# Turning the second half's rows with VectorE in 32x32 blocks instead of TensorE transposes

## What is computed

```python
h = concatenate([meta, x])                                     # 16 meta tokens ahead of 2048
m = pool_mixer(h, a_w_in, a_w_group, a_scale, a_w_out)
h = layer_norm(ALPHA * h + m, ln_mix_g, ln_mix_b)
h = layer_norm(ALPHA * h + swiglu_ffn(h, ffn_w_gu, ffn_w_down), ln_ffn_g, ln_ffn_b)
return h[:, N_META:]

def swiglu_ffn(x, w_gu, w_down):
    gate, up = split(x @ w_gu, 2)      # 1024 -> 2816 each
    return (silu(gate) * up) @ w_down
```

## Time and profile before

| what | value |
|---|---|
| median of 3 runs | 1648.08 us |
| profiled execution | 1648.43 us |
| span of its instructions | 1646.5 us |
| TensorE busy | 1637.0 us (99%) |
| VectorE busy | 1036.0 us (63%) |
| GpSimd busy | 642.5 us (39%) |
| ScalarE busy | 620.9 us (38%) |
| mean granted TensorE clock | 0.999 of full |

### The profile page before, as it was taken

The page is one execution under the profiler, slowest core; times in us unless marked ns, Lnnn a source line. Parts: engine busy times, 40 slices in busy tenths (PEclk is TensorE's granted clock), DMA queues, the critical chain, the costliest instruction groups (busy, mean ns, idle before and its releaser), DMA issues.

```text
span 1646.5 us, 19031 instructions
## 1 busy us (share of the span) xinstructions
PE 1637.0 (99%) x7302; PEld 1354.2 (82%) x7302; DVE 1036.0 (63%) x1083; ACT 620.9 (38%) x844; POOL 642.5 (39%) x440
## 2 busy tenths in 40 slices
PE   9999999999999999999999999999999999999998
PEld 7888888888888888888888888888888888888886
DVE  6878885998445444454756677766643443467866
ACT  6334454445433433433533333333343332322330
POOL 0430025116357666654455666666621000341000
PEclk9999999999999999999999999999999999999999
DMA  9674467534467566565756666666577543564542
GB/s 361 250 284 154 152 252 261 193 141 177 120 212 239 190 209 224 181 198 192 243 181 222 216 211 192 203 209 200 176 222 275 188 146 131 196 223 173 197 146 95
DMA packets 190954, 330.84 MB, mean 201 GB/s; under 512 B 8464, under 2 KB 132496, under 8 KB 181136
## 3 DMA queue, kind: packets, MB, share of 16 engines
q1 hardware_dynamic: 151168, 297.64, 52.6%
q10 hardware_dynamic: 37520, 23.60, 4.7%
q0 software_dynamic: 2176, 8.39, 1.3%
HBM read 227.36 MB, written 102.24 MB: 200 GB/s over the span
## 4 chain that ended last, share of the span: by engine, by line
PE 97%; DVE 1%; DMA 0%; issue 0%; SPq 0%; ACT 0%; DVEq 0%
PE acc L1237 44%; PE acc L1269 19%; PE acc L1072 11%; PE turn L1237 7%; PE turn L1269 6%; PE acc L1106 6%; PE turn L1106 2%; PE acc L1136 1%; PE turn L1060 1%; PE acc L1149 0%; DMA raw<-w_out 0%; DVE fa L1846 0%; DVE split L1673 0%; DVE zm L1772 0%; DVE ring L1754 0%
## 5 line engine op out<-in xcount | busy, mean ns | idle before, releaser
L1237 PE MATMUL acc<-fa,wf 128*128 128x512 f32 x1584 | 366.1, 390 | 0.0
L1237 PE MATMUL acc<-fb,wf 128*128 128x512 f32 x1584 | 362.9, 389 | 0.0
L1237 PEld LDWEIGHTS acc<-fb,wf 128*128 128x128 f32 x1584 | 297.2, 188 | 62.0 <-issue 0.3
L1237 PEld LDWEIGHTS acc<-fa,wf 128*128 128x128 f32 x1584 | 296.1, 188 | 61.3 <-issue 0.2
L1269 PE MATMUL acc<-dw,da 128*128 128x512 f32 x1386 | 315.3, 389 | 0.0
L1269 PEld LDWEIGHTS acc<-dw,da 128*128 128x128 f32 x1386 | 260.1, 188 | 54.0
L1853 DVE TENSOR_TENSOR wf<-wt,wf 128x512 fp32r<-128x512 f32 x132 | 132.2, 1004 | 158.3 <-ACT wf L1442 158.2
L1853 DVE TENSOR_TENSOR wf<-wr,wf 128x512 fp32r<-128x512 f32 x176 | 171.8, 981 | 52.8 <-ACT wf L1442 52.5
L891 POOL TENSOR_TENSOR wt<-wr,wt 128x512 f32<-128x512 f32 x88 | 138.2, 1570 | 167.4 <-DVE wf L1853 167.3
L1442 ACT CAST wf<-wr 128x512 fp32r<-128x512 f32 x176 | 108.7, 618 | 212.5 <-PE acc L1237 200.6
L1947 DVE TENSOR_TENSOR da<-dar,da 128x1408 fp32r<-128x1408 f32 x56 | 91.9, 1642 | 136.3 <-ACT da L1556 136.3
(11 more groups left out here) (144 smaller groups left out, 1800.4 us busy)
## 6 DMA issues: line engine op xcount, KB each, us to landing
wr<-w_gu SPq DMA_DIRECT2D x44, 1024.0 KB, 5.2
dar<-af_dram SPq DMA_DIRECT2D x56, 704.0 KB, 4.3
af_dram<-g ACTq DMA_DIRECT2D x32, 512.0 KB, 5.7
raw<-w_in SPq DMA_DIRECT2D x15, 1024.0 KB, 7.0
fs<-hf_dram SPq DMA_DIRECT2D x14, 1024.0 KB, 5.9
dt_raw<-w_down SPq DMA_DIRECT2D x22, 512.0 KB, 5.6
wt_dram<-dt_t SPq DMA_DIRECT2D x22, 512.0 KB, 3.5
sa<-af_dram SPq DMA_DIRECT2D x22, 512.0 KB, 8.4
```

What stands on the lines that cost most here:

```text
L1237: mm = nc.tensor.matmul(dst, wf[:, slot, a, k, :], fa[half][i][:, v, :, k, :], start=i < 2 and k == 0 and n3 == 0, stop=k == KC - 1 and n3 ...
```

## The change

- The second half's rows are no longer transposed by TensorE. VectorE transposes them in blocks of 32x32 (`turn_rows`): four instructions of 128x512 elements for a pair, in the pair's first unit (5, 8, 11, 14), behind `unit_lo(n + 1, 0)` and, in an even unit, behind `up_out`. Each reads `nat_gu` with a step of 8 elements and writes straight into `st_gu`.
- A 32x32 transpose leaves a block on its own 32 partitions. So the rows are loaded such that partition group q holds column quarter q of 32 rows: 8 DMAs of 128 KB for a pair, with 1 KB pieces, in place of 2 of 512 KB with 4 KB pieces.
- The inner index that lands on a partition is then 8 * partition + chunk instead of 128 * chunk + partition. The host lays the gate and up weights and the norm's gain and bias out in that order (`by_chunks`). The first half is still transposed by TensorE, and reads its rows with a step of 8 elements, too (`pair_rows`).
- ScalarE's gain and bias are applied in place in `st_gu` (`scale_turned`), two activations of 128x256 at the same two places of the same units as `take_turn` had.
- `turn_rows` takes over the waits for the rows (`pair_landed`), for the store of the pair before (`st_stored`) and for its sums (`ss_made`).

```diff
--- before.py
+++ after.py
@@ -60,6 +60,9 @@
         return MIX0 + h * HALF_CHUNKS + 2 * PAIRS + t
 
     ADDS = HALVES * TT
+    Q = 32
+    QT = P // Q
+    assert QT == 4 and D // QT == KT * Q
 
     x_rows = x.rearrange("(n p) d -> p n d", p=P)
     h_rows = h_dram.rearrange("(n p) d -> p n d", p=P)
@@ -111,7 +114,7 @@
 
         st_mix = [at(f"st_mix{n}", R0 + off * KB, [P, 4, KC, P]) for n, off in enumerate((72, 88))]
         ss_mix = at("ss_mix", R0 + 96 * KB, [P, 4, KC, P])
-        nat_gu = at("nat_gu", N0, [P, 2, D])
+        nat_gu = at("nat_gu", N0, [P, 2, QT, D // QT])
         st_gu = at("st_gu", Z0, [P, 4, KC, P])
         ss_gu = at("ss_gu", Z0 + 8 * KB, [P, 4, KC, P])
 
@@ -373,11 +376,15 @@
         def st_of(pi):
             return st_mix[pi % 2] if pi < 4 else st_gu
 
-        def pair_rows(pi, a):
-
-            if pi >= TT:
-                return nat_gu[:, a]
-            return zm[a][:, pi]
+        def pair_rows(pi, a, kk):
+
+            return zm[a][:, pi].rearrange("p (r c) -> p c r", c=KT)[:, kk]
+
+        def turned_block(n):
+
+            a, kh = ((1, 0), (0, 0), (0, 1), (1, 1))[n]
+            src = nat_gu[:, a].rearrange("p g (r c) -> p g c r", c=KT)[:, :, kh * KC:(kh + 1) * KC]
+            return st_gu[:, n].rearrange("p k (g t) -> p g k t", t=Q), src
 
 
         HF_OF = (0, 3, 4, 1, 5, 6, 2)
@@ -561,9 +568,11 @@
                         for row in range(TT):
                             sp.wait_ge(rows_stored[e][row], 2 * 16)
                 else:
-                    sp.wait_ge(turn_done, 4 * pi)
+                    sp.wait_ge(turn_done, TT * pi)
+                src = h_dram.rearrange("(h a j g t) (q c) -> h j a g q t c", h=2, a=2, j=TT, g=QT, q=QT)[half, j]
                 for a in range(2):
-                    sp.dma_start(nat_gu[:, a, :], h_rows[:, half * 2 * TT + a * TT + j, :]).then_inc(pair_landed, 16)
+                    for n in range(QT):
+                        sp.dma_start(nat_gu[:, a, n], src[a, n]).then_inc(pair_landed, 16)
 
             def load_form(q):
                 half, i = form_of(q)
@@ -1047,18 +1056,12 @@
             def turn_part(pi, k):
 
                 part = TT * pi + k
-                if k == 0 and pi < TT:
+                if k == 0:
                     pe.wait_ge(normed, TT + pi + 1)
-                elif k == 0:
-                    pe.wait_ge(pair_landed, 32 * (pi - TT + 1))
-                slot = k % 2 if pi < TT else 1
-                if pi < TT and part >= 2:
+                if part >= 2:
                     pe.wait_ge(turn_taken, 2 * (part - 1))
-                elif pi >= TT:
-                    pe.wait_ge(turn_taken, 2 * part)
                 for n, (a, kk) in enumerate(((1, k), (0, k), (0, KC + k), (1, KC + k))):
-                    mm = nc.tensor.transpose(turn[:, slot, n * P:(n + 1) * P], pair_rows(pi, a)[:, kk * P:(kk + 1) * P],
-                                             ident[:])
+                    mm = nc.tensor.transpose(turn[:, k % 2, n * P:(n + 1) * P], pair_rows(pi, a, kk), ident[:])
                 mm.then_inc(turn_done, 1)
 
             def hidden(c, x_of, slot, banks, before=None, between=None):
@@ -1242,8 +1245,6 @@
             for n in range(UNITS):
                 for i in range(NP):
                     product(n, i)
-                    if turned_in(n)[0] is not None and i in (1, 4):
-                        turn_part(turned_in(n)[0], turned_in(n)[1] + i // 4)
 
             for k in range(DSTEPS):
                 t, m = k // MT, k % MT
@@ -1306,26 +1307,36 @@
                 if k == 0 and pi < 2:
 
                     act.wait_ge(d_lo_ready, NP)
-                if k == 0 and pi >= TT:
-                    act.wait_ge(st_stored[(pi - 1) % 2], 16 * ((pi + 1) // 2))
-                    act.wait_ge(ss_made, 4 * pi)
-                elif k == 0 and pi >= 2:
+                if k == 0 and pi >= 2:
 
                     act.wait_ge(st_stored[pi % 2], 16 * (pi // 2))
                     act.wait_ge(ss_made, 4 * (pi - 1))
-                slot = k % 2 if pi < TT else 1
                 if part == 0:
                     act.wait_ge(mix_gb_landed, 32)
 
                 for n, kk in enumerate((k, KC + k)):
                     nc.scalar.activation(st_of(pi)[:, 2 * n:2 * n + 2, k, :],
-                                         turn[:, slot, 2 * n * P:2 * (n + 1) * P].rearrange("p (b t) -> p b t", t=P),
+                                         turn[:, k % 2, 2 * n * P:2 * (n + 1) * P].rearrange("p (b t) -> p b t", t=P),
                                          ACT.Identity, bias=mix_b_sb[:, kk:kk + 1], scale=mix_g_sb[:, kk:kk + 1]
                                          ).then_inc(turn_taken, 1)
                 if k == KC - 1:
-                    act.wait_ge(turn_taken, 2 * (part + 1))
-                    nc.scalar.dma_start(pair_forms(pi)[:, 0:3, :], st_of(pi)[:, 1:4].rearrange("p f k t -> p f (k t)")
-                                        ).then_inc(st_stored[pi % 2], 16)
+                    store_turned(pi)
+
+            def store_turned(pi):
+                act.wait_ge(turn_taken, 2 * TT * (pi + 1))
+                nc.scalar.dma_start(pair_forms(pi)[:, 0:3, :], st_of(pi)[:, 1:4].rearrange("p f k t -> p f (k t)")
+                                    ).then_inc(st_stored[pi % 2], 16)
+
+            def scale_turned(pi, step):
+
+                kh, ks = step // 2, (2 * (step % 2), 2 * (step % 2) + 1)
+                act.wait_ge(turn_done, TT * pi + 2 * (kh + 1))
+                for k in ks:
+                    both, kk = st_gu[:, 2 * kh:2 * kh + 2, k, :], kh * KC + k
+                    nc.scalar.activation(both, both, ACT.Identity, bias=mix_b_sb[:, kk:kk + 1],
+                                         scale=mix_g_sb[:, kk:kk + 1]).then_inc(turn_taken, 1)
+                if step == 3:
+                    store_turned(pi)
 
             def stage_u(b, i):
                 act.wait_ge(chunk_done, c_in(b, i) + 1)
@@ -1599,7 +1610,7 @@
                     for j in LAST_ROWS[2 * (n - 2):2 * (n - 1)]:
                         norm(LAST, j)
                 if turned_in(n)[0] is not None:
-                    take_turn(turned_in(n)[0], turned_in(n)[1])
+                    scale_turned(turned_in(n)[0], turned_in(n)[1])
                 if n == 0:
                     unit_hi(1, 0)
                     unit_hi(1, 1)
@@ -1629,7 +1640,7 @@
                         down_w_hi(v)
                     act_form_hi(1)
                 if turned_in(n)[0] is not None:
-                    take_turn(turned_in(n)[0], turned_in(n)[1] + 1)
+                    scale_turned(turned_in(n)[0], turned_in(n)[1] + 1)
                 if gate:
                     act.wait_ge(c22_made, n + 1)
                     gate_out(jj, 3, g_of(jj)[:, 3, :])
@@ -1957,6 +1968,15 @@
                 if (n, place) in FORM_LO:
                     form_lo(FORM_LO[n, place])
 
+            def turn_rows(pi):
+
+                dve.wait_ge(pair_landed, 16 * 2 * QT * (pi - TT + 1))
+                dve.wait_ge(st_stored[(pi - 1) % 2], 16 * ((pi + 1) // 2))
+                dve.wait_ge(ss_made, 4 * pi)
+                for n in range(4):
+                    dst, src = turned_block(n)
+                    nc.vector.transpose(dst, src).then_inc(turn_done, 1)
+
             for n in range(UNITS):
                 jj, gate, nxt = n // 2, n % 2 == 0, n + 1 < UNITS
 
@@ -1966,6 +1986,8 @@
                 if n and gate:
                     dve.wait_ge(prod_done, NP * n)
                     up_out(jj - 1, 1, bank(n - 1, 1))
+                if turned_in(n)[1] == 0:
+                    turn_rows(turned_in(n)[0])
                 if n and nxt:
                     unit_lo(n + 1, 1)
                     new_form(n, 1)
@@ -2169,7 +2191,11 @@
     n_meta, ff, kt, cp = inputs["meta"].shape[0], inputs["ffn_w_down"].shape[1], d // P, CW // P
     jf = ff // (2 * P)
 
-    w_gu = np.asarray(inputs["ffn_w_gu"]).reshape(2, kt // 2, P, 2, 2, jf, P).transpose(0, 4, 5, 3, 2, 1, 6)
+    def by_chunks(a):
+
+        return np.asarray(a).reshape(P, 2, kt // 2, -1).transpose(1, 2, 0, 3)
+
+    w_gu = by_chunks(inputs["ffn_w_gu"]).reshape(2, kt // 2, P, 2, 2, jf, P).transpose(0, 4, 5, 3, 2, 1, 6)
 
     w_down = np.asarray(inputs["ffn_w_down"]).reshape(2, jf, P, 2, d // 2).transpose(0, 3, 2, 1, 4)
     arrays = {
@@ -2186,8 +2212,8 @@
         "w_out": lay(inputs["a_w_out"], (GROUPS, cp, P, d), (0, 2, 1, 3)),
         "mix_g": np.ascontiguousarray(inputs["ln_mix_g"][0]),
         "mix_b": np.ascontiguousarray(inputs["ln_mix_b"][0]),
-        "mix_gt": lay(inputs["ln_mix_g"], (kt, P), (1, 0)),
-        "mix_bt": lay(inputs["ln_mix_b"], (kt, P), (1, 0)),
+        "mix_gt": lay(by_chunks(inputs["ln_mix_g"]), (kt, P), (1, 0)),
+        "mix_bt": lay(by_chunks(inputs["ln_mix_b"]), (kt, P), (1, 0)),
 
         "w_gu": np.ascontiguousarray(blocks(w_gu).transpose(1, 2, 3, 0, 4, 5)),
```

## The result

The changed kernel takes 1660.82 us, the median of 6 runs (1660.33 to 1661.67), against 1648.32 us for the kernel before in its 6: ratio 1.0074, 95% interval 1.0064 to 1.0085. It is slower by 12.5 us, where 1641.0 was forecast. The profiled execution took 1660.33 us, its span is 1658.5 us (before: 1648.43 and 1646.5).

A forecast was written before the change was run, and what follows sets the result against it. TensorE, busy 1637.0 of 1646.5 us, was taken to bound the kernel. 1648.43 - 7.8 removed + 0.5 lateness = 1641.1 us, 1640.8 for the median, stated as 1641.0; range 1639.8 to 1650.0 us.

The forecast's parts named there:

- What bounds the kernel: Whole kernel: TensorE, busy 1637.0 of 1646.5 us, sets the time; other engines matter only through their dates.
- what is removed: TensorE's path: eight units lose their two parts of four transposes, 0.97 us each, 7.8 us in all.
- VectorE's transposes: Units 5, 8, 11, 14: four 128x512 transposes each, 0.7 to 1.2 us apiece, fit in VectorE's gaps.
- the seed's date: Product 4, 10.88 us into the unit, needs VectorE's seed; in time up to 1.76 (unit 5) or 1.18 us (unit 8) per transpose.
- 1.24 us for a transpose: VectorE: upper estimate from the skill's page for a 128x512 transpose; the sum about 0.8 us worse than at 0.7 us.
- The first half's transposes: TensorE: 64 transposes stay, now read with a step of 8; cost taken as nothing, upper bound 7.6 us.
- Rival B: TensorE: strided loads double the transposes' distance, 0.109 to 0.218 us; 7.0 us come back, 1648.0 us; chance 0.22.
- The rows' arrival: SP's eight loads: issues about 6.1 us, landing 4.4 us; pair 4 at 475.2 us, 2.8 us behind VectorE.
- all lateness: Units with VectorE's new work: 0.5 us in all allowed in the sum.
- Rival D: Row loads land late: pair 4 at 479.8 us, its seed 3.1 us late; 1643.6 us; chance 0.13.
- Rival C: VectorE too slow: 2.46 us per strided transpose, seed late in units 5, 8, 11, 14; 1656.6 us; chance 0.15.

The follow-up runs named there:

- the kernel with the later transposes: Changed kernel with each pair's four VectorE transposes moved behind the seed and unit_lo(n + 1, 3), ScalarE's scalings later still: 1644.55 us, ratio 0.9976.

## Why the prediction was wrong

- **What bounds the kernel, and what is removed**: right. With rows in time the kernel takes 1640.95 us, 7.5 us under the kernel before; 7.8 less 0.5 was worked out, 1641.0 forecast.
- **VectorE's transposes**: right. 0.7 to 1.2 us was taken, 1.05 to 1.16 measured, and the seed's date held: limits of 1.76 and 1.18 us. At 1.24 us for a transpose, though, the prediction's own dates give some 1.2 us of loss and not 0.8: 0.7 in unit 5, whose rows are late, and 0.2 in units 8 and 14 each.
- **The first half's transposes**: the choice of nothing was right (64 times 0.002 us more by the distances, 0.1 us). The reason given spoke of a read side with room; each load did become longer, by 52 ns, and only the distance hardly did. Rival B, a doubled distance, is refuted (the transposes stand at 221 to 266 us, not from 204 as it says). The Trainium skill's rule on cachelines ("Advanced Engine Details and Errata", section "SBUF Cachelines"), weighed there, agrees with both engines at a step of 32 bytes: 1.7 times the time of a transpose on VectorE, 1.4 times that of a load on TensorE. Only steps of 1 and 8 elements were run, so that the line of 16 bytes itself is not shown.
- **The rows' arrival is the step that failed.** "8 take about 6.1 us", and another 4.4 us or so to landing, gave 475.2 us for pair 4 and no harm later. Measured: 7.7 us for the issues and rows at 481.3; for pairs 5 to 7 the issues took 10.5 to 13.0 us and the rows were 3.3 to 5.9 us late, where they were to be in time. The sum had 0.5 us for all lateness; it was 19.1 us, the waits with what followed them. The prices came from rows of DMAs whose source is 128 rows deep. The new ones have the column quarter, 4, outermost, and run on a quarter of the engines. The working looked at number and size and not at the order of the source's dimensions, although the diff shows it.
- **Rival D** named the right wait and the right place, and was given 0.13 and 1643.6 us. It failed in size: it took the old landing as the worst case, counted a loss at pair 4 alone, and had no term for the clock. Issues of 12.4 us for eight, which it put aside as the exception, are about what pairs 5 to 7 had. Four stalls of 12.3 us in all brought another 6.2 us at 1.2 GHz.
- **Rival C** came nearest in time, 1656.6 us, by luck: its reason, transposes of 2.46 us, is refuted by the 1.05 to 1.16 us measured.

## What to carry to other kernels

Before moving a load to a new layout, read the order of its dimensions on both sides: the outermost one should be 16 or a multiple (16, 32 and 128 were quick here, 2 and 4 slow). Where a layout needs a small outer dimension, loop over it and give each DMA the rows. In a profile, a flat stretch of the DMA share at 1 or 2 tenths with an even, low rate is the mark of it. And a wait put into a full engine's stream should be priced at the worst arrival, with the low clock that followed the stalls of 3.0 to 5.1 us here.

## What the runs showed of the hardware that was not expected

- The rate of a DMA by its outermost dimension: 49 GB/s at 2, 95 to 100 at 4, and the issue itself lengthens, 2.63 and 1.23 us in the median against 0.60 at 16 and 0.43 at 32 and 128.
- A load on few engines leaves a backlog in which a store that ScalarE issues took 15.5 us, where the same store took 8.0 before and 7.0 with quick loads.
- Transposing 128x512 float32 in blocks of 32x32 takes VectorE 0.67 us with step 1 and 1.13 us with step 8.
- A weight load with step 8 takes 192 ns in place of 140, with transposes still 0.111 us apart in place of 0.109.
- A stall of 3.0 us was followed by the clock's low level for some us (1.5 us lost), one of 0.69 us was not. The loss doesn't follow the stall's length alone: behind 3.5 us in the kernel with the later transposes 24 matmuls took 8.33 us in place of 5.6, 2.7 us lost, behind 3.6 us in the changed kernel 1.7 us.
